# Cached memory keys turned by VectorE and fetched through DRAM instead of by TensorE

## The reference, cut to what matters

```
cache_mem_k: (DEPTH 2, DEC_BATCH 8, N_MEM 256, MEM_HEADS 4, MEM_HEAD_DIM 128)

def _mem_attend(h, mk, mv, w_q, w_o):
    q = (h @ w_q).reshape(n, length, MEM_HEADS, MEM_HEAD_DIM)
    sc = jnp.einsum('nlhd,nmhd->nhlm', q, mk).astype(jnp.float32) * (MEM_HEAD_DIM ** -0.5)
    p = jax.nn.softmax(sc, axis=-1).astype(mv.dtype)
    o = jnp.einsum('nhlm,nmhd->nlhd', p, mv).reshape(n, length, MEM_DIM)
    return o @ w_o

x = x + _pool_mix(u_ext, t, pool_w_group[l], pool_scale[l]) @ pool_w_out[l]
x = x + _mem_attend(_rmsnorm(x, norm_mem_q[l]), mem_k[l], mem_v[l], mem_w_q[l], mem_w_o[l])
x = x + _swiglu(_rmsnorm(x, norm_ffn[l]), ffn_w_gate[l], ffn_w_up[l], ffn_w_down[l])
```

## Time and profile before

| | us |
|---|---|
| median of 3 runs (lowest, highest) | 2319.57 (2318.7, 2320.48) |
| the profiled execution: its own time | 2319.61 |
| its span in the trace | 2317.8 |
| TensorE busy | 2296.9 (99%) |
| VectorE busy | 1351.7 (58%) |
| ScalarE busy | 953.2 (41%) |
| GpSimd busy | 165.9 (7%) |

### The profile page before, as it was taken

The page is one execution under the profiler, slowest core; times in us unless marked ns, Lnnn a source line. Parts: engine busy times, 40 slices in busy tenths (PEclk is TensorE's granted clock), DMA queues, the critical chain, the costliest instruction groups (busy, mean ns, idle before and its releaser), DMA issues.

```text
span 2317.8 us, 45899 instructions
## 1 busy us (share of the span) xinstructions
PE 2296.9 (99%) x19062; PEld 2268.1 (98%) x19062; DVE 1351.7 (58%) x1729; ACT 953.2 (41%) x1135; POOL 165.9 (7%) x186
## 2 busy tenths in 40 slices
PE   9999999999999999999999998999999999999999
PEld 8999998999999999999999997899999999999999
DVE  7778557655446565455656767675554455544554
ACT  7434455433333333334444334553333333333343
POOL 0100112000001211000110111110000000000001
PEclk9999999999999999999999999999999999999999
DMA  8655765655557888555565675655555555555553
GB/s 292 197 195 179 241 199 185 191 177 179 181 181 231 246 247 249 181 177 179 171 199 174 201 228 164 219 164 179 176 179 181 181 177 178 179 181 182 177 170 126
DMA packets 387128, 445.89 MB, mean 192 GB/s; under 512 B 14762, under 2 KB 350906, under 8 KB 386494
## 3 DMA queue, kind: packets, MB, share of 16 engines
q1 hardware_dynamic: 373902, 401.72, 53.2%
q0 software_dynamic: 12592, 42.14, 6.3%
q10 hardware_dynamic: 528, 0.52, 0.1%
HBM read 432.50 MB, written 12.74 MB: 192 GB/s over the span
## 4 chain that ended last, share of the span: by engine, by line
PE 98%; DVE 1%; ACT 0%; DMA 0%; DVEq 0%; issue 0%; POOL 0%; ACTq 0%; POOLq 0%
PE acc L788 31%; PE acc L790 30%; PE acc L789 30%; PE acc L865 1%; PE acc L873 1%; PE acc L866 1%; PE ab L1045 0%; PE acc L998 0%; PE acc L967 0%; PE acc L977 0%; PE ab L884 0%; PE ab L967 0%; PE ab L934 0%; PE ab L1081 0%; DMA att<-in_norm_ffn 0%; PE ab L1103 0%
## 5 line engine op out<-in xcount | busy, mean ns | idle before, releaser
L788 PE MATMUL acc<-xs,whi 128*128 128x264 f32 (+1 forms) x3776 | 1081.3, 286 | 0.0
L790 PE MATMUL acc<-xs,wlo 128*128 128x264 f32 (+1 forms) x3776 | 1073.1, 284 | 0.0
L789 PE MATMUL acc<-xs,whi 128*128 128x264 f32 (+1 forms) x3776 | 1072.1, 284 | 0.0
L477 ACT ACTIVATE whi<-raw 128x1024 fp32r<-128x1024 f32 x744 | 763.9, 1056 | 708.5 <-DMA raw<-in_ffn_w_up 286.1
L1305 DVE TENSOR_TENSOR wlo<-raw,whi 128x1024 fp32r<-128x1024 f32 x744 | 879.6, 1233 | 201.7 <-ACT whi L477 181.6
L790 PEld LDWEIGHTS acc<-xs,wlo 128*128 128x128 f32 x3776 | 713.1, 189 | 0.0
L788 PEld LDWEIGHTS acc<-xs,whi 128*128 128x128 f32 x3776 | 709.2, 188 | 2.0 <-issue 1.1
L789 PEld LDWEIGHTS acc<-xs,whi 128*128 128x128 f32 x3776 | 710.7, 188 | 0.2
L788 PE MATMUL acc<-hA,whi 128*128 128x264 f32 (+1 forms) x1216 | 347.7, 286 | 1.5 <-DVE hA L1594 1.0
L790 PE MATMUL acc<-hA,wlo 128*128 128x264 f32 (+1 forms) x1216 | 346.4, 285 | 0.0
L789 PE MATMUL acc<-hA,whi 128*128 128x264 f32 (+1 forms) x1216 | 345.7, 284 | 0.0
(11 more groups left out here) (285 smaller groups left out, 1147.5 us busy)
## 6 DMA issues: line engine op xcount, KB each, us to landing
raw<-in_ffn_w_gate SPq DMA_DIRECT2D x176, 512.0 KB, 3.4
raw<-in_ffn_w_up SPq DMA_DIRECT2D x176, 512.0 KB, 3.5
raw<-in_ffn_w_down SPq DMA_DIRECT2D x176, 512.0 KB, 3.4
raw<-in_dil_w_q SPq DMA_DIRECT2D x48, 512.0 KB, 4.1
raw<-in_pool_w_in SPq DMA_DIRECT2D x32, 512.0 KB, 3.4
raw<-in_pool_w_out SPq DMA_DIRECT2D x32, 512.0 KB, 3.4
raw<-in_mem_w_v SPq DMA_DIRECT2D x16, 512.0 KB, 8.3
raw<-in_mem_w_k SPq DMA_DIRECT2D x16, 512.0 KB, 5.7
```

The lines of the kernel that those rows point to most:

```text
L477: nc.scalar.activation(half_block(whi, n, half), half_block(raw, n, half), ACT.Copy).then_inc(hi_ready, 1)
L788: mm(out, w_hi, hi_, start=first, stop=False)
L789: mm(out, w_hi, lo_, start=False, stop=False)
L790: return mm(out, w_lo, hi_, start=False, stop=last)
```

## The change

The transposes on TensorE and the copies on ScalarE are taken out. The memory keys take the way through DRAM: `turn_memory_rows(l, i)` loads the rows of two samples (1 MB) into the first half of `kx`, VectorE turns the 32 by 32 blocks into the second half, `store_memory_rows` writes them with four DMAs to `m_turned`, in runs of 32 floats, and `load_memory_keys` fetches them, key dimension on the partitions, with four DMAs of 256 KB per pair of samples, in runs of 128 floats. There is one buffer for rows and one for turned rows; the load of the next pair waits for the stores of the one before. Layer 0 is turned in items 0 to 3 of wout, layer 1 in turns 4 to 7 of part 0 of the first FFN. Keys are fetched so: pairs 0 and 2 of layer 0 after item 4 of wout, pairs 1 and 3 when mq0 starts; in layer 1 pairs 0 to 2 when the mixer's heads are done, pair 3 when mq1 starts.

`turn_keys(b)` on TensorE and `memory_keys_turned(l, b)` on ScalarE are deleted, with `load_first_keys`. The diff's pieces are TensorE's, then VectorE's in wout and in a turn of the FFN's gate part, then GpSimd's:

```diff
                 def sample_scores(q):
                     eng.wait_ge(qz_ready, l + 1)
-                    eng.wait_ge(kt_free, k0 + TS)
+                    for i in (2 * q, 2 * q + 1):
+                        eng.wait_ge(memory_keys_in[i], 64 * (l + 1))
...
-                pair_item(n, g, 2, xtile, xs_wait(f"memq{l}"), after_first=lambda: statistics(f"memq{l}"),
-                          halves={b: lambda b=b: turn_keys(b) for b in range(4)})
+                pair_item(n, g, 2, xtile, xs_wait(f"memq{l}"), after_first=lambda: statistics(f"memq{l}"))
                 pair_item(n + 2, g + 1, 2, xtile,
-                          halves={0: lambda: (scores(0), scores(1)), 1: lambda: turn_keys(4),
-                                  2: lambda: (turn_probabilities(0), turn_keys(5)), 3: lambda: turn_keys(6)})
+                          halves={0: lambda: (scores(0), scores(1)), 2: lambda: turn_probabilities(0)})
                 weigh(0)
-                turn_keys(7)
                 turn_probabilities(1)
...
                 low_tiles("memq0", 2 * j)
+                if j < 4:
+                    eng.wait_ge(rows_landed, 16 * j + 16)
+                    v.transpose(memory_rows_turned, memory_rows_in).then_inc(keys_blocked, 1)
...
                         split_h(h, t, upF)
                         eng.drain()
+                        if l == 0 and part == 0 and h is hB:
+                            eng.wait_ge(rows_landed, 16 * i + 16)
+                            v.transpose(memory_rows_turned, memory_rows_in).then_inc(keys_blocked, 1)
...
+            def turn_memory_rows(l, i):
+                count = 4 * l + i
+                if count:
+                    eng.wait_ge(keys_stored, 64 * count)
+                src = a["cache_mem_k"][l, 2 * i:2 * i + 2]
+                eng.dma_start(memory_rows_in.rearrange("p (b k c) -> p b k c", b=2, k=2),
+                              src.rearrange("b (k p) h d -> p b k (h d)", p=P)).then_inc(rows_landed, 16)
+            def store_memory_rows(l, i):
+                eng.wait_ge(keys_blocked, 4 * l + i + 1)
+                rows = m_turned[(4 * l + i) * BLK:(4 * l + i + 1) * BLK, :].rearrange("(x t) (j s) -> t j x s", t=32, s=32)
+                for j in range(4):
+                    eng.dma_start(rows[:, j], quadrant(memory_rows_turned, j).rearrange("t (x s) -> t x s", s=32)).then_inc(keys_stored, 16)
+            def load_memory_keys(l, i):
+                for b in (2 * i, 2 * i + 1):
+                    for k in range(2):
+                        at = (4 * l + i) * BLK + (2 * (b % 2) + k) * MEMD
+                        eng.dma_start(KTm(b)[:, :, k * P:(k + 1) * P],
+                                      m_turned[at:at + MEMD, :].rearrange("(h d) j -> d h j", d=P)).then_inc(memory_keys_in[i], 16)
...
-            load_first_keys(0)
-            add_squares("memq0")
+            turn_memory_rows(0, 0)
+            for j in range(8):
+                if j:
+                    eng.wait_ge(sq_ready, j + 1)
+                    gp.tensor_tensor(ssq[:, :, :], ssq[:, :, :], sq[:, :, :], ALU.add).then_inc(sq_added, 1)
+                    eng.drain()
+                if j < 4:
+                    store_memory_rows(0, j)
+                if j < 3:
+                    turn_memory_rows(0, j + 1)
+                if j == 4:
+                    eng.wait_ge(keys_stored, 64 * 4)
+                    load_memory_keys(0, 0)
+                    load_memory_keys(0, 2)
...
             add_squares("ffn0")
+            for i in range(4):
+                turn_memory_rows(1, i)
+                store_memory_rows(1, i)
...
-            load_first_keys(1)
+            eng.wait_ge(h_ready, H0["m1"])
+            for i in range(3):
+                load_memory_keys(1, i)
```

More of the change, by code:

```diff
@@ L84 @@
 for _l in range(2):
-    CACHED += [((f"mk{_l}", i), s) for i, s in enumerate((9, 10, 5, 9))]
     CACHED += [((f"mv{_l}", i), s) for i, s in enumerate((0, 1, 2, 3))]
@@ L173, in sample_values_at @@
             return home, at + b * P
+        memory_rows_in, memory_rows_turned = kx[:, 0:BLK], kx[:, BLK:2 * BLK]
+        m_turned = nc.dram_tensor("m_turned", (2 * 4 * BLK, P), F32, kind="Internal").ap()
         rows_in, rows_turned = kx[:, 0:NG * MEMD], kx[:, NG * MEMD:2 * NG * MEMD]
@@ L253, in trunk @@
         scored = sem("scored")
-        kt_ready, kt_free = sem("kt_ready"), sem("kt_free")
+        memory_keys_in = [sem(f"memory_keys_in{i}") for i in range(4)]
         qz_ready = sem("qz_ready")
@@ L548, in high_items @@
                         upto(N0[f"mo{l}"] + min(i + 3, 5))
-            def memory_keys_turned(l, b):
-                eng.wait_ge(kt_ready, KT0[f"m{l}"] + b + 1)
-                src = ab[:, 0:2, :] if b < 4 else acc[:, 2 * (G0[f"mq{l}"] % 2):2 * (G0[f"mq{l}"] % 2) + 2, :]
-                nc.scalar.copy(KTm(b).rearrange("p h j -> p (h j)"), src.rearrange("p b c -> p (b c)")).then_inc(kt_free, 1)
             def memory_queries(l):
-                n = N0[f"mq{l}"]
-                memory_keys_turned(l, 0)
-                upto(n + 2)
-                memory_keys_turned(l, 1)
+                upto(N0[f"mq{l}"] + 2)
                 root(STAT[f"memq{l}"])
-                upto(n + 3)
-                memory_keys_turned(l, 2)
-                memory_keys_turned(l, 3)
+                upto(N0[f"mq{l}"] + 3)
             def mem_attention(l):
@@ L581, in mem_attention @@
                 head_exp(1)
-                memory_keys_turned(l, 4)
                 upto(mo + 1)
-                for b in range(5, TS):
-                    memory_keys_turned(l, b)
                 head_exp(2)
@@ L923, in mem_attention @@
                 n, g = N0[f"mq{l}"], G0[f"mq{l}"]
-                h0, k0 = H0[f"m{l}"], KT0[f"m{l}"]
+                h0 = H0[f"m{l}"]
                 sc, vo = 2 * (g % 2), 2 * ((g + 1) % 2)
@@ L953, in weigh @@
                     last.then_inc(o_ready, 1)
-                def turn_keys(b):
-                    key = (f"mk{l}", b // 2)
-                    cached_landed(eng, key)
-                    if b == 4:
-                        eng.wait_ge(acc_free, g + 1)
-                    elif b:
-                        eng.wait_ge(kt_free, k0 + b)
-                    rows = cached(key).rearrange("p (b k c) -> p b k c", b=2, k=2)
-                    for h in range(NH_MEM):
-                        for k in range(2):
-                            j = 2 * h + k
-                            dst = (ab[:, j // 4] if b < 4 else acc[:, sc + j // 4])[:, (j % 4) * P:(j % 4 + 1) * P]
-                            last = nc.tensor.transpose(dst, rows[:, b % 2, k, h * P:(h + 1) * P], ident[:, :])
-                    last.then_inc(kt_ready, 1)
                 def sample_scores(q):
                     eng.wait_ge(qz_ready, l + 1)
-                    eng.wait_ge(kt_free, k0 + TS)
+                    for i in (2 * q, 2 * q + 1):
+                        eng.wait_ge(memory_keys_in[i], 64 * (l + 1))
                     for h in range(NH_MEM):
@@ L1972, in taken @@
                 eng.wait_ge(acc_free, g + 1)
+            def turn_memory_rows(l, i):
[16 more added lines that the diff above has]
+                                      m_turned[at:at + MEMD, :].rearrange("(h d) j -> d h j", d=P)).then_inc(memory_keys_in[i], 16)
             def load_memory_rows(l):
                 eng.wait_ge(half_used, 2 * N0[f"mq{l}"])
-                load_cached(eng, (f"mk{l}", 2))
-                eng.wait_ge(kt_ready, KT0[f"m{l}"] + 2)
-                load_cached(eng, (f"mk{l}", 3))
+                for i in (3,) if l else (1, 3):
+                    load_memory_keys(l, i)
                 eng.wait_ge(half_used, 2 * (N0[f"mq{l}"] + 4))
@@ L1982, in load_memory_rows @@
                     load_cached(eng, (f"mv{l}", i))
-            def load_first_keys(l):
-                if l == 0:
-                    eng.wait_ge(stored[0], STORED[2])
-                    eng.wait_ge(stored[1], STORED[3])
-                else:
-                    eng.wait_ge(h_ready, H0["m1"])
-                for i in range(2):
-                    load_cached(eng, (f"mk{l}", i))
             def quadrant(rows, j, first=0, n=32):
```

14 lines of the change are left out of this document (6 added, 8 removed).

## The result

The changed kernel takes 2337.7 us (median of 4 runs, 2332.89 to 2338.07) against 2319.14 us before (4 runs, 2318.13 to 2320.48): ratio 1.0075, with a 95% interval of 1.0063 to 1.0087. It is slower by 0.75%. The forecast was 2332.1 us, slower, with a range of 2316 to 2343 us. The profiled run took 2332.89 us (span 2330.7); it is the shortest of the four.

What follows compares the result with a forecast made beforehand. TensorE, busy 99% of the span, was taken to bound the kernel: 2319.6 - 11.4 (turns removed) + 20.6 (delay in wout) + 1.8 (lower clock) + 1.5 (third pair of keys) = 2332.1 us, range 2316 to 2343.

Steps and rivals of the forecast that it cites:

- The circle, C = 21.1: One round in wout: turn 2.4, to the issue 0.2, four stores 11.0, load to next turn 7.5 us.
- The delay, 20.6 + 1.8: In wout TensorE gets block 11 20.6 us late; the lower clock after the last wait costs 1.8 us.
- The waits, 1.8, 9.4 and 9.4 us: In wout TensorE waits for blocks 7, 9 and 11, whose splits are queued on VectorE behind waiting turns.
- only eats into the second: Lower clock after the first 9.4 us wait in wout only shortens the next; after the last it costs.
- waits of only 3 to 5 us for a cheaper leg of stores: Sign in the trace: if TensorE's waits in wout last 3 to 5 us, the stores' leg was priced wrong.
- The gain, 11.4 us: TensorE's turns gone in both layers' memory attention: 12 x 0.87 + 2 x 0.5 us, between 10.4 and 13.9.
- turns 6 and 7: Last turns before the values in each layer's attention: together give 0.5 us in place of 1.74, values limit.
- The third pair in "do", 1.5 us: Layer 1's mixer output: 3 MB of keys instead of 2 delays weights; item 2's addition late for item 4.
- Layer 1's turns cost nothing: First FFN, part 0: turns come every 23.4 us, so 21.1 us a round still fits.
- The short circle, C under 14.2: Rival in wout: turns hidden, gain arrives whole; with a round of 15.2 us, 2312.6 us; chance 0.11.
- The rival in between, 17 to 19 us: Rival in wout: shorter rounds as TensorE idles in later ones; 2321.0 us, no difference; chance 0.13.
- The Trainium skill's formula: About 2.0 us plus bytes over 436 GB/s per GpSimd transfer: load 4.4, four stores about 6.3 us; kernel 2309.7 us.

Runs made afterwards that it cites:

- Experiments 4: Changed kernel with layer 0's turns in items 0, 2, 4 and 6 of wout and its fetches moved behind them: 2317.83 us, ratio 0.9996.
- 6: Changed kernel with GpSimd's drains in the second half of the pooling output replaced by waits for its own additions: 2337.29 us, ratio 1.0084.
- 7: Changed kernel with a second buffer for rows, turns still in items 0 to 3: 2318.29 us; the same without the drains: 2313.76 us.
- after_again: The changed kernel once more, no edit: 2336.53 us, ratio 1.0075 to the kernel before.
- layer0_only: Changed kernel with only layer 0's keys going the new way, layer 1's turned by TensorE as before: 2342.1 us, ratio 1.0095.
- layer 1 alone: Changed kernel with layer 0 as in the kernel before, only layer 1 the new way: 2321.31 us, ratio 1.0006; run again 2317.03 us, ratio 1.0001.

## Why the prediction was right

The median is inside the range and the kernel is slower, as forecast; it is 5.6 us above the number, while the profiled run is 0.8 us above. Step by step:

- **The circle, C = 21.1.** It was 21.1 on average in the first profile. That it fits so closely is in part luck, since the legs' errors cancel: stores 10.6 instead of 11.0, loads 7.9 instead of 7.5, and 2.6 from a turn's start to the issue, as assumed. Experiments 4, 6 and 7 show that this is the cause: with the same bytes spread over twice the time wout loses nothing, with shorter circles it loses 5 to 7 us, and without the drain it loses as much as before.
- **The mis-sized term is the circle of the usual run.** In `after_again` it was 66.5 / 3 = 22.2 us and in `layer0_only` 22.4. My range for it, 19.5 to 23.5, holds both; the value that I took was that of the shortest of the four runs. 3 x 1.1 = 3.3 us is most of what the median has over the forecast. In `after_again` the stores take 12.9, 10.3 and 10.1 us, 11.1 on average, as I had taken them. The loads take 9.1, 8.0 and 8.4 us, 8.5 on average, where I had taken 7.5 from the row of a load that was alone. Why the legs are longer in one run than in another of the same kernel stays open.
- **The delay, 20.6 + 1.8.** Measured 24.05. The missing 1.7 us are the start: the first turn ended at 250.4, not 248.7. I had taken the first load to be there after 9.2 us, when VectorE has made the low tiles of item 0. It took 11.1.
- **The waits, 1.8, 9.4 and 9.4 us.** They were 5.61, 6.50 and 4.77. The first was larger by the late start and the longer first circle. Behind it TensorE worked at 0.50 for much of the next item, so that it reached its next wait later. I had said that this "only eats into the second". That was right for the sum and wrong for what is to be seen. So the sign that I had named, waits of only 3 to 5 us for a cheaper leg of stores, would have misled: waits of about 5 us came with a circle of 21.1. The distance between the turns tells the circle, the length of the waits doesn't. After the last wait 3.25 us busy at 0.50, at 0.22 instead of 0.12 us a matmul, cost 3.25 x 0.10 / 0.22 = 1.5 us, where I had 1.8.
- **The gain, 11.4 us.** Measured 6.7 + 4.9 = 11.6, but the layers aren't alike, as I had said they were (5.7 us each). In layer 0 the first six turns gave 5.2 us and turns 6 and 7 another 1.5, nearly the whole 1.74 where I had taken 0.5: TensorE waits only 0.46 us among the values' matmuls (at 386.29). In layer 1 the six gave 4.7 and the last two 0.2, since there the values do come too late. That the sum fits is luck. The wait in layer 1:

```profile
1517.22 1.06 PE L968 MATMUL acc<-xs_flat,tmp 128*4 128x128 f32 x32 [1.70 <-DMA xs_flat<-in_cache_mem_v]
```

- **The third pair in "do", 1.5 us.** Measured +1.6, but one item later than named. I had expected the addition of item 2 to come late for item 4. It was in time, at 1447.51, 12.6 us into the phase where before it stood 13.3 us into it. The wait stands at the start of item 5, 168 matmuls into the phase, for the addition of item 3, since ScalarE had waited 2.60 and 2.87 us for the next two weight halves (at 1450.28 and 1454.21):

```profile
1456.45 0.70 DVE L1327 TENSOR_TENSOR x<-acc,x 128x528 f32<-128x528 f32 x1
1457.20 0.39 PE L774 MATMUL acc<-hA,whi 128*128 128x264 f32 x1 [1.33 <-DVE x L1327]
```

- **Layer 1's turns cost nothing.** Right: they come 23.2 to 23.9 us apart (533.65, 557.06, 580.95, 604.19), with 0.18 to 0.67 us of idle time before each, and layer 1 alone costs nothing in the FFN.
- **The rivals.** The short circle, C under 14.2, would have made the change pay. With two buffers it wasn't quite reached (14.1 to 15.9 us for turn and stores alone); what paid was to ask for the circle every 23 us and to take the drain out. The rival in between, 17 to 19 us, didn't come about: the shortest of three rounds was 19.1 us. The Trainium skill's formula ("DMA: Bandwidth & Descriptors", section "Anatomy of one DMA"), by which the circle was estimated at 13.3 us and the time at 2309.7, doesn't hold beside weight loads: four stores took 9.6 to 12.3 us, a load of 1 MB 6.9 to 11.1 us.

## What to carry to other kernels

Before moving work off the busiest engine, write down the circle that the new way goes through (turn, store, load) and compare it with the time between two uses, not its engines' busy time: here it was 21.1 us against 11.7, and it was hidden wherever it had 23 us. Look next at what is queued behind the wait on the same engine, since that is what the bottleneck will wait for. When a wait on the critical path goes and the time doesn't fall by as much, look in the profile for the next one before calling the change useless: the paced version gained nothing until a drain of GpSimd had gone too. In the kernel before, with no transfer of its own in flight, GpSimd's last addition followed the drain after 0.16 us.

## What was not expected of the hardware

- **A drain on GpSimd waits for GpSimd's transfers in flight.** Four stores issued by 324.29 us held the next addition until 331.90 us, 0.3 us behind the landing of the last, and a load held it for 4.5 to 5.5 us in each of three other places, also until it had landed. With a semaphore wait in place of the drain, and the same stores in flight, it followed after 0.1 us.
- **An addition on GpSimd and VectorE's work beside it can hold each other, and either can lose.** Beside a run of four subtractions of 128x1024 elements it took 6.11 us in one profile, and ended 1.2 us after the last of them, while they took their usual 1.21 us each. In the other profile of the same kernel it took 1.60 us, and the first subtraction 2.35 us. It started 0.33 to 0.34 us ahead of them both times. What decides who waits isn't settled here. The other additions of that stage take 1.3 us, and 2.37 us where one lies beside two subtractions. The Trainium skill, "GPSIMD Engine Reference", section "Architecture", says that GpSimd's read and write ports are shared with VectorE. The traces agree with that, but a run that takes the subtractions away wasn't made.
- **The lower clock comes in stretches of 3.4, 6.8 or 10.2 us** around the ends of waits of 2.2 to 9 us, and not the same from run to run in the same kernel (6.8, 6.8 and 3.4 against 10.2, 6.8 and 6.8 us). What chooses the length isn't settled here.
- **The same transfers and turns took 63.4 us for three rounds in one run and 66.5 us in another** of the same kernel. This, more than the clock, is what parts its two profiled runs, which are 4.4 us apart; runs of the kernel before differ by 2 to 3 us.
